# A 64-expert MoE loop on one core: one pick of a group's common expert, and hidden rows turned by VectorE and ScalarE

## The reference, cut to what matters

```python
scores = sigmoid(x @ router_w)                       # (576, 64)
# 4 of 8 groups of experts, then the best 8 experts in them, per row
gates  = normalised scores of the 8 chosen * 2.5     # 0 elsewhere
hb     = silu(x @ ex_w1[e]) * (x @ ex_w3[e])         # (rows, 256), for each of 64 experts
routed = sum over e of (hb * gates[:, e]) @ ex_w2[e] # (rows, 1024)
```

## Time and profile before

| | |
|---|---|
| runs | 1022.7, 1023.09, 1023.42 us; median 1023.09 |
| the profiled execution's own time | 1023.74 us, its span 1022.0 us |
| granted TensorE clock, mean over the span | 0.989 |
| TensorE busy (matmuls / weight loads) | 975.8 us (95%) / 436.6 us (43%) |
| VectorE, ScalarE, GpSimd busy | 452.9, 146.4, 352.1 us |
| DMA, of the span | 297.54 MB, mean 291 GB/s |
| the loop of 46 steps | from about 343 to about 923 us |

### The profile page before, as it was taken

How to read it: one execution, slowest core, us unless ns; L and a number is a source line. 1 busy time by engine, 2 the same in 40 slices (tenths; PEclk the granted TensorE clock), 3 DMA queues, 4 the chain that set the end, 5 groups by cost and what they waited for, 6 DMA issues and landing times.

```text
span 1022.0 us, 16640 instructions
## 1 busy us (share of the span) xinstructions
PE 975.8 (95%) x6109; PEld 436.6 (43%) x6109; DVE 452.9 (44%) x1319; ACT 146.4 (14%) x358; POOL 352.1 (34%) x439
## 2 busy tenths in 40 slices
PE   7999999999999899999999999899997899999996
PEld 5777555655545333333333333233332233333442
DVE  3411221344568634444443434444434443442885
ACT  4000023301022000010001010001000001112332
POOL 6000331300043644442543434444433344440232
PEclk9999999999999999999999999999998999999999
DMA  8033224222076989999999999999999999988932
GB/s 282 2 94 104 83 74 119 101 63 73 21 247 262 387 327 377 406 412 400 412 411 411 408 409 416 411 408 407 413 403 393 383 413 400 409 329 337 421 134 83
DMA packets 76118, 297.54 MB, mean 291 GB/s; under 512 B 15622, under 2 KB 26062, under 8 KB 49149
## 3 DMA queue, kind: packets, MB, share of 16 engines
q1 hardware_dynamic: 60133, 258.68, 64.8%
q0 software_dynamic: 15904, 37.79, 9.6%
HBM read 276.56 MB, written 31.50 MB: 301 GB/s over the span
## 4 chain that ended last, share of the span: by engine, by line
PE 73%; DMA 12%; DVE 5%; issue 4%; POOL 3%; DVEq 1%; another core or an unknown queue 1%; SPq 0%; ACT 0%; POOLq 0%; ACTq 0%
PE bank L2331 26%; PE bank L1982 22%; PE bank L2326 8%; PE bank L2429 5%; DMA arena<-xs_dram,slot 5%; DMA arena<-in_ex_w 3%; DMA ring<-in_ex_w 3%; PE bank L1988 2%; POOL arena L988 2%; PE bank L2381 1%; PE bank L2159 1%; PE bank L2086 1%; PE bank L2076 1%; PE bank L2123 1%; DMA x<-in_x_prompt 1%
## 5 line engine op out<-in xcount | busy, mean ns | idle before, releaser
L2331 PE MATMUL bank<-arena 128*32 128x512 f32 x1440 | 272.5, 596 | 2.7 <-DMA ring<-in_ex_w 1.9
L988 POOL DMA_INDIRECT arena<-xs_dram,slot x192 | 210.5, 1096 | 73.2 <-issue 62.8
L2331 PE MATMUL bank<-ring,arena 128*32 128x512 f32 x864 | 214.9, 604 | 3.4 <-DMA arena<-in_ex_w 2.2
L1004 POOL DMA_INDIRECT y_dram<-arena,outrow x46 | 47.1, 1023 | 267.5 <-DVE slot L1773 218.8
L2331 PE MATMUL bank<-xT,arena 128*32 128x512 f32 x576 | 115.3, 607 | 5.2 <-DMA ring<-in_ex_w 5.2
L2331 PEld LDWEIGHTS bank<-arena 128*32 128x32 f32 x1440 | 72.1, 110 | 99.2 <-issue 93.3
L1982 PE MATMUL bank<-xT,ring 128*128 128x288 f32 x384 | 93.4, 406 | 0.0
L1787 DVE STREAM_TRANSPOSE arena<-arena 128x1024 f32<-128x1024 f32 x48 | 59.7, 1244 | 73.1 <-DMA arena<-xs_dram,slot 68.7
L2331 PE MATMUL bank<-mixpj,arena 128*32 128x512 f32 x384 | 84.7, 594 | 0.0
L1982 PEld LDWEIGHTS bank<-xT,ring 128*128 128x128 f32 x384 | 72.9, 190 | 20.5 <-DMA ring<-in_w_in 0.5
L1852 DVE SCALAR_TENSOR_TENSOR arena<-bank,gate,arena 128x256 f32<-128x256 f32 x46 | 22.3, 484 | 128.3 <-ACT arena L1198 119.9
(11 more groups left out here) (422 smaller groups left out, 1269.0 us busy)
## 6 DMA issues: line engine op xcount, KB each, us to landing
arena<-in_ex_w SPq DMA_DIRECT2D x78, 1024.0 KB
ring<-in_ex_w SPq DMA_DIRECT2D x50, 1024.0 KB
xT<-in_ex_w SPq DMA_DIRECT2D x28, 1024.0 KB
mixpj<-in_ex_w SPq DMA_DIRECT2D x24, 1024.0 KB
arena<-y_dram SPq DMA_DIRECT2D x18, 1024.0 KB, 10.7
wide<-in_ex_w SPq DMA_DIRECT2D x12, 1024.0 KB
ring<-in_w_in SPq DMA_DIRECT2D x5, 2048.0 KB, 9.3
ring<-in_w_out SPq DMA_DIRECT2D x2, 2048.0 KB, 8.8
```

Source lines behind the costliest of these rows:

```text
L988: pool.indirect_dma_start(xg[b][:, 256 * a:256 * a + 256], None, xs_quarter, bass.IndirectOffsetOnAxis(slot[k][:, a:a + 1], 0), bounds_che ...
L1004: pool.indirect_dma_start(y_dram, bass.IndirectOffsetOnAxis(outrow[b][:, 0:1], 0), og[b], None, bounds_check=K * T - 1, oob_is_err=False). ...
L2331: ins = pe.matmul(b[t, :], lhs[:, t], rhs(home(own if lane < 3 else common)), start=start, stop=stop)
```

## The change

Part one: a group's common expert is compared and picked once. In turn 0 of a group P `one_hot_common` builds the 0/1 matrix of the common expert with all three of its lanes, and the pick writes columns for lane 3 of turns 0, 1 and 2 side by side into bank 7; turn t writes its own 18 columns from column 6t, so that they end where the common expert's columns for turn t lie, and `index` reads 24 columns from 6t. Turns 1 and 2 build and pick their own expert alone. Steps Q are as before, but the common part is built first. The tiles `inqx` and `valqx` lie where `hits` was.

Part two: the two TensorE transposes and the ScalarE copy out of bank 4 go. VectorE transposes `hh` in 32x32 blocks into `hz` (the tile `hu`), and ScalarE moves the 16 blocks to their places in `hT` with 16 copies of 32 partitions x 64 elements. VectorE waits for `s_hT` of the step before, and TensorE now waits for `s_h` of the step before ahead of mm1(j).

```diff
+        hz = hu.rearrange("p (c k t) -> p c k t", c=2, t=LANE)
...
+        def joins(j):
+
+            return kind(j) == "Q" or (kind(j) == "P" and turn_of(j) == 0)
...
             # ScalarE, step j
-                    act.wait_ge(s_pht, base + (j + 1))
-                    act.copy(hT, bank[4][:, 0:2 * P].rearrange("p (c t) -> p c t", t=P)).then_inc(s_hT, 1)
+                    act.wait_ge(s_z, base + (j + 1))
+                    for a in range(4):
+                        for k in range(4):
+                            ins = act.copy(hT[LANE * k:LANE * k + LANE, :, LANE * a:LANE * a + LANE],
+                                           hz[LANE * a:LANE * a + LANE, :, k, :])
+                    ins.then_inc(s_hT, 1)
...
+            def one_hots(base, mixed, j, own, common):
+
+                if joins(j):
+                    w, lanes = (3, iotam[:, :]) if kind(j) == "P" else (2, iotar[:, :])
+                    one_hot_common(mixed + SHARED[j + 1], common, w, lanes)
+                w, lanes = {"S": (4, iotaq[:, :]), "P": (3, iotam[:, :]), "Q": (2, iotar[:, :])}[kind(j)]
+                one_hot(base + (j + 1), j % 2, own, w, lanes).then_inc(s_onehot, 1)
+
+            def index(at, k, b, t, done):
+
+                got = b[:, 6 * t:6 * t + 24].rearrange("p (a c) -> p a c", c=6)
...
             # VectorE, step j, behind hh (L1852)
+                    if j:
+                        dve.wait_ge(s_hT, base + j)
+                    dve.wait_ge(s_h, base + (j + 1))
+                    dve.transpose(hz, hh.rearrange("p (k i c) -> p c k i", k=4, c=2)).then_inc(s_z, 1)
...
             # TensorE
+            def pick(at, b, out, j, common):
+
+                t, w = turn_of(j), LANES[kind(j)]
                 pe.wait_ge(s_onehot, at)
                 for i in range(NT):
+                    ins = pe.matmul(out[:, 6 * t:6 * t + 6 * w], match32[b][:, i].rearrange("p q j -> p (q j)"),
+                                    valq[b][:, i, 0:w].rearrange("p a c -> p (a c)"), start=(i == 0),
                                     stop=(i == NT - 1))
+                if common:
+                    wx = 3 if kind(j) == "P" else 2
+                    for i in range(NT):
+                        ins = pe.matmul(out[:, 6 * (w + t):6 * (w + wx)], matchx[:, i].rearrange("p q j -> p (q j)"),
+                                        valqx[:, i, t:wx].rearrange("p a c -> p (a c)"), start=(i == 0),
+                                        stop=(i == NT - 1))
                 return ins
...
             # TensorE, step j
+                    if j:
+                        pe.wait_ge(s_h, base + j)
                     pe.wait_ge(s_xgT, base + (j + 1))
...
+                    pick(base + (j + 4), (j + 3) % 2, bank[7], j + 3, joins(j + 3) or j == 0).then_inc(s_psel, 1)
                     if j:
                         mm2(base, r, j - 1)
-                    pe.wait_ge(s_h, base + (j + 1))
-                    for c in range(2):
-                        ins = pe.transpose(bank[4][:, P * c:P * c + P], hh[:, c:FF:2], ident[:, :])
-                    ins.then_inc(s_pht, 1)
```

More of the change, by code:

```diff
@@ L355, in decoder_step @@
         matchx = matchx_raw.bitcast(BF16).rearrange("p (i q j) -> p i q j", q=4, j=32)
-        inqx = ex(NT * 2).rearrange("p (i a) -> p i a", a=2)
-        valqx = ex(NT * 2 * 6 // 2).bitcast(BF16).rearrange("p (i a c) -> p i a c", a=2, c=6)
-        rank_row, keys, hits = (ex(NE)[0:NE, :] for _ in range(3))
+        rank_row, keys = (ex(NE)[0:NE, :] for _ in range(2))
+        hits_raw = ex(NE)
+        hits = hits_raw[0:NE, :]
+        inqx = hits_raw[:, 0:NT * 3].rearrange("p (i a) -> p i a", a=3)
+        valqx = hits_raw[:, NT * 3:NT * 3 + NT * 3 * 6 // 2].bitcast(BF16).rearrange("p (i a c) -> p i a c", a=3, c=6)
         np_k, np_c = keys[0:1, :].bitcast(I32), rank_row[0:1, :]
@@ L448, in decoder_step @@
         (s_cols, s_inq, s_onehot, s_index, s_picked, s_gate, s_h, s_xgT, s_out1, s_silu, s_hT, s_out0,
-         s_psel, s_mm1, s_pht, s_mm2) = (sem(n) for n in (
+         s_psel, s_mm1, s_z, s_mm2) = (sem(n) for n in (
              "s_cols", "s_inq", "s_onehot", "s_index", "s_picked", "s_gate", "s_h", "s_xgT", "s_out1", "s_silu",
-             "s_hT", "s_out0", "s_psel", "s_mm1", "s_pht", "s_mm2"))
+             "s_hT", "s_out0", "s_psel", "s_mm1", "s_z", "s_mm2"))
         s_y8 = [[sem(f"s_y8_{b}{q}") for q in range(4)] for b in range(2)]
@@ L541, in decoder_step @@
         for j in range(2 * STEPS):
-            SHARED.append(SHARED[-1] + shares(j))
+            SHARED.append(SHARED[-1] + joins(j))
         def bc(dram_row, n=P):
@@ L1858, in step @@
                     dve.wait_ge(s_psel, base + (j + 1))
-                    index(base + (j + 4), depth(j + 3), bank[7], lambda ins: None)
+                    index(base + (j + 4), depth(j + 3), bank[7], turn_of(j + 3), lambda ins: None)
                     turned_rows(rows + (j // 2 + 2) * 64, j % 2)
-                    e = [expert(p) for p in places(j + 4)]
-                    if shares(j + 4):
-                        one_hot_shared(base + (j + 5), mixed + SHARED[j + 5], j % 2, e[0], e[1], j + 4)
-                    else:
-                        one_hot(base + (j + 5), j % 2, e[0])
+                    own, common = (places(j + 4) + [None])[0:2]
+                    one_hots(base, mixed, j + 4, expert(own), expert(common) if joins(j + 4) else None)
                 for j in range(STEPS):
@@ L2266, in _ @@
             first(2, 4, KT)
-            def pick(at, b, out):
+            def pick(at, b, out, j, common):
+                t, w = turn_of(j), LANES[kind(j)]
                 pe.wait_ge(s_onehot, at)
                 for i in range(NT):
-                    ins = pe.matmul(out[:, 0:24], match32[b][:, i].rearrange("p q j -> p (q j)"),
-                                    valq[b][:, i].rearrange("p a c -> p (a c)"), start=(i == 0), stop=(i == NT - 1))
-                return ins
-            def pick_shared(at, b, out, j):
-                w = LANES[kind(j)]
-                pe.wait_ge(s_onehot, at)
-                for i in range(NT):
-                    pe.matmul(out[:, 0:6 * w], match32[b][:, i].rearrange("p q j -> p (q j)"),
-                              valq[b][:, i, 0:w].rearrange("p a c -> p (a c)"), start=(i == 0), stop=(i == NT - 1))
-                for i in range(NT):
-                    ins = pe.matmul(out[:, 6 * w:24], matchx[:, i].rearrange("p q j -> p (q j)"),
-                                    valqx[:, i, 0:4 - w].rearrange("p a c -> p (a c)"), start=(i == 0),
-                                    stop=(i == NT - 1))
+                    ins = pe.matmul(out[:, 6 * t:6 * t + 6 * w], match32[b][:, i].rearrange("p q j -> p (q j)"),
+                                    valq[b][:, i, 0:w].rearrange("p a c -> p (a c)"), start=(i == 0),
+                                    stop=(i == NT - 1))
+                if common:
[4 more added lines that the diff above has]
+                                        stop=(i == NT - 1))
                 return ins
@@ L2290, in first_pick @@
                 b = free_bank(pe, "pk", j)
-                if shares(j):
-                    pick_shared(j + 1, j % 2, b, j).then_inc(filled, 1)
-                else:
-                    pick(j + 1, j % 2, b).then_inc(filled, 1)
+                pick(j + 1, j % 2, b, j, j > 0).then_inc(filled, 1)
             first_pick(0)
```

53 lines of the change are left out of this document (16 added, 37 removed).

## The result

The changed kernel takes 1028.3 us, the median of 6 runs (1026.77 to 1031.25); 6 runs of the kernel before on the same chip gave 1022.89 (1022.18 to 1024.38). The ratio is 1.0044, with a 95% interval from 1.0024 to 1.0064. So the change costs 2.5 to 6.5 us. The profiled execution took 1029.28 us, its span is 1027.5 us and its mean granted clock 0.975 (before: 1023.74, 1022.0 and 0.989).

What follows compares the result with a forecast made beforehand. The prediction took the loop as bound by DMA, the queue of weights, from 387 to 907 us, TensorE close behind. Terms -1.7 + 2.7 - 0.7 + 2.2 = +2.5 us on the median 1023.09 gave 1025.6 us, range 1018.5 to 1029.5.

Steps and rivals of the forecast that it cites:

- Loop bound by DMA; 27.3 us of TensorE returned to the queue: Loop, 387 to 907 us: the weights' queue sets the pace, so TensorE's 27.3 us less work becomes waits for weights.
- Rival B: Faster, chance 0.18: homes freed sooner speed the queue, say 1019 us; far end, TensorE the bound all along, 998.5 us (0.03).
- -1.7 us for an earlier full queue: Loop start, 350 to 387 us: homes freed sooner start transfers up to 1.7 us sooner, and all later ones inherit that.
- +2.7 us for the 16 copies: Loop end: copies take 3.5 us in place of 0.4 ahead of the last mm2; VectorE gives back 0.4; net +2.7 us.
- -0.7 us for the landing: Behind the loop: the last scatter lands 0 to 2.7 us faster, gate weights being further on; a quarter taken, -0.7 us.
- +2.2 us for one fall of the clock: Last mm1 or mm2: longer TensorE waits drop its clock to half; one loss of 2.2 us taken, bounds 0 and 4.4.
- VectorE's transpose at no cost: Each step: the 128x256 transpose takes at most 0.31 us on VectorE, hidden while the copy of bank 6 awaits mm2.
- Part one worth nothing of itself: Turns 1 and 2: fewer picks save TensorE 3.4 us, and this relief is returned to the queue of weights.
- Rival A: Chance 0.32: as forecast, but the clock holds or the scatter's landing absorbs the delay; +0.3 us, 1023.4 us.
- Rival C: Chance 0.05: ScalarE copies from 0.41 us each hold up every step; at 0.5 us each, 41 us slower, 1064 us.

Runs made afterwards that it cites:

- The halved loads: Kernel before and changed kernel, each first-layer weight transfer in the loop bringing half its matrix: 993.55 and 986.01 us, ratios 0.9700 and 0.9622 to the kernel before.
- early_turned: Kernel before with part one in all steps and part two in steps 0 to 7 alone: ratio 0.9995 to the kernel before.
- turned_only: Kernel before with part two alone (block transposes and 16 copies in every step), picks as they were: ratio 1.0045, 4.6 us.
- before_last_turned: Kernel before with part two in the last step alone: ratio 1.0025 to the kernel before, +2.6 us.
- last_by_tensor: Changed kernel with TensorE's transposes and one ScalarE copy back in the last step alone: ratio 1.0028 to the kernel before, +2.9 us.
- one_pick: Kernel before with part one alone, hidden rows still turned by TensorE and copied once: ratio 0.9984 to the kernel before, 0.9978 when run again.
- last_by_tensor_fill: last_by_tensor with 18 unread 128x128 matmuls put ahead of the last mm1: ratio 1.0007 to the kernel before.
- dead_transposes: Changed kernel with the two TensorE transposes still made in every step and read by nobody: ratio 1.0036 to the kernel before.
- filler: Changed kernel with five unread 128x512 matmuls between mm2 of step 44 and the last mm2: ratio 1.0034 to the kernel before.

## Why the prediction was right, and where it was off

The forecast was 1025.6 us, slower, in a range from 1018.5 to 1029.5; measured 1028.3. By the ratio the loss is 4.5 us (2.5 to 6.5) where the sum said 2.5. The mechanism held for the end of the loop: bare copies and one fall of the clock. For the loop itself it did not; there I had forecast a small gain, and part two loses 2 to 4.5 us in it. Link by link, the profiles differ from the sum by +3.9 us at the last mm1, +0.6 at the copies, -2.2 at the landing, -0.2 at the clock and +1.0 ahead of the gate. That the size stayed near the forecast is in part luck, for the landing took back much of what the loop lost.

- **Loop bound by DMA; 27.3 us of TensorE returned to the queue.** Right in the main. TensorE's busy time fell by 30.7 us over the span and the DMA share stayed at 1.01. Its waits rose by some 20 us for weights and 12 us at the picks, which the sum had left out. The halved loads show the same: without the wait for weights only 10.6 us of the 27.3 come through, since picks and gathers are next. Rival B's far end, 998.5 us, needed all of them.
- **-1.7 us for an earlier full queue.** This is the step that failed. The queue was fuller from 350 to 387 us, 0.96 and 363 GB/s in place of 0.90 and 336, as the step says. But "all later ones inherit that" is not borne out. The changed kernel began to issue the last first-layer weights 5.3 us sooner than the kernel before (876.05 in place of 881.37 us), and used them 2.2 us later:

```profile
876.05 4.75 SPq L667 DMA_DIRECT2D mixpj<-in_ex_w  x2
```

```profile
909.33 0.61 PE L2323 MATMUL bank<-xT,arena 128*64 128x512 f32 x1 [1.87 <-issue]
```

They lay 33.3 us in place of 25.8 between the start of the issues and the use, and the pair of issues itself took 4.75 us in place of 1.11. So in this queue, full as it was, a home freed sooner brought no weights sooner. 1.5 us of the 2.2 were there before the loop (first mm1 at 344.71 in place of 343.20), and such differences come between executions of one kernel too. What counts is the set of ratios: `early_turned` gained nothing, and part two in steps 0 to 44 costs 2.0 us (`turned_only` against `before_last_turned`) or 4.5 us (`last_by_tensor` against `one_pick`). The term should have been a loss of some 2 us or more.
- **+2.7 us for the 16 copies.** Mis-sized by a little: the copies took 4.07 us in place of the 3.5 taken, so the net is +3.3. A copy costs 244 ns and the next starts 0.25 us behind it; my row had 0.23 us for one of 64 elements in four. The 0.4 us back from VectorE came, 0.44.
- **-0.7 us for the landing.** Mis-sized: -2.85 us, past the bound of -2.7. The queue was emptier while the scatter landed (DMA share 0.47 from 932 to 937 us, where it was 0.67 from 925 to 932), and it landed in 3.99 us. 0.96 us went again before the gate's first matmul.
- **+2.2 us for one fall of the clock.** The last mm2: +2.0 us. But I counted one fall and had bounded two at 4.4. `last_by_tensor` shows the second, +2.6 us in its last mm1, and filling the wait ahead of it brought some 2 us. In the changed kernel's own profile that second fall came one step sooner, at 894.80 (8.78 us in place of 7.09), where the wait of 1.87 us ahead of the last mm1 took it in. Every profile of a kernel whose last step is turned by VectorE and ScalarE, without a filler, pays for one fall (its last mm2 takes 5.2 to 6.3 us). Some executions may pay for the other too, and a part of the gap between 2.5 and 4.5 us can lie there; no run here shows how often.
- **VectorE's transpose at no cost.** It took 0.45 us, over the 0.31 taken and under the bound, and was covered.
- **Part one worth nothing of itself.** Wrong by 2 us: 0.9984 and 0.9978. I had returned all of its relief to the queue of weights; 1.2 us of it is seen behind the last mm1, where the queue no longer decides.
- **Rival A** (clock holds, 0.32): no, the clock fell. **Rival B** (faster, 0.18): no for the change, but part one alone went there. **Rival C** (0.05): no, 244 ns a copy, and even twice the copies cost 20 us, not 40 and more.

The Trainium skill, page VectorE: DVE Perf Modes, section Rules for kernel authors, recommends TensorE for a 128x128 transpose whose result may lie in PSUM, and by that rule part two had to lose. `turned_only` agrees, at 1.0045. The reason is not VectorE's price, though, which stayed hidden: it is the 16 copies that lay bare behind the last step, a TensorE that stands idle longer before the pieces of work that nothing covers, and a loss in the loop that is only in part explained.

Open is what is left of the loop's half: `last_by_tensor_fill` and part one alone differ by 0.2 to 0.3%, 2 to 3 us, and `dead_transposes` seems to lose as much with its clock up. One candidate was only seen, not tested. In the table of DMA queues from 387 to 925 us, the changed kernel fetches more instructions in one queue. The changed kernel, and then part one alone, second run:

```profile
q14 instruction: 25, 0.20, 0.1%
```

```profile
q14 instruction: 18, 0.15, 0.1%
```

The rows here show no engine by itself. Against the candidate stands `early_turned`: it has 19 packets, one more than part one alone, and yet lost 1.9 us to it. A kernel with fewer and larger ScalarE instructions in the loop would tell.

## What to carry to other kernels

Work that a loop hides is bare in the last step: price each moved piece there, not only in the steady state, and keep the short path for the last iteration. When an engine is relieved under another bound, ask where its new waits fall; a wait ahead of uncovered work costs its clock as well. Test the parts of a change alone: here one part alone was worth 2 us and the other alone cost 4.6.

## What the runs showed of the hardware

- The ScalarE copy of 32x64 f32 took 244 ns in SBUF and 208 ns into PSUM, 16 of them 4.07 us; the copy of 128x256 f32 out of PSUM, sixteen times the data of one, took 0.38 us. Over so few elements the time goes by the number of copies.
- TensorE's granted clock was 0.57 from 910 to 917 us, near the lower level of 1.2 GHz, behind a wait of 3.75 us, and 1.00 when 18 matmuls of `ident` (36 in the profile, 4.02 us) filled the wait. In the profiles these matmuls that compute nothing brought the last mm1 from 9.73 to 7.02 us; five larger ones brought the changed kernel's last mm2 from 5.67 to 3.67 us (`filler`). What they bring to the whole, 2 and 1 us by the ratios, is within the noise.
- A scatter of the same size landed in 3.99 us when it came 7 us later into an emptier queue (DMA share 0.47), in place of 6.84 us (share 0.67); in the profiles of `turned_only` and `filler`, where it came as late, in 3.94 and 4.13 us.
- With the queue full, first-layer weights whose issue began 5.3 us sooner were used 2.2 us later: 33.3 us from issue to use in place of 25.8.
